# Transposes of the values placed between fill chunks, one gate chunk and the convolution taps placed anew, in the two sparse layers

## The reference, cut to what matters

```python
def second_block(x, meta_tokens, w_in, conv_w, conv_b, conv_ln_g, conv_ln_b, w_out, post_ln_g, post_ln_b):
    ...
    for l in range(DEPTH_2):                                   # 2 layers, 272 tokens, width 1024
        proj = jnp.einsum('bld,de->ble', h, w_in[l])
        a, g, zc, q, k, v, za, qi, ki, wi = jnp.split(proj, IN_SPLITS, axis=-1)
        y_conv = conformer_conv_branch(a, g, zc, ...)           # 31 taps per channel, layer norm, silu, * silu(zc)
        q, k, qi, ki = (rope of each)
        y_attn = dsa_sparse_attention(q, k, v, qi, ki, wi, topk) * jax.nn.silu(za)   # 68 best keys of each query
        y = jnp.einsum('ble,ed->bld', jnp.concatenate([y_conv, y_attn], axis=-1), w_out[l])
        h = layer_norm(DEEPNORM_ALPHA * h + y, post_ln_g[l], post_ln_b[l])
```

## Time and profile before

| what | value |
|---|---|
| median of the three timed runs | 986.49 us (986.46, 988.08, 986.49) |
| profiled execution, its own time | 985.01 us |
| its span, first to last instruction | 982.9 us |
| PE busy | 904.8 us, 92% of the span |
| POOL busy | 616.8 us, 63% |
| DVE busy | 518.4 us, 53% |
| ACT busy | 474.6 us, 48% |
| share of PE in the chain that ended last | 78% |

### The profile page before, as it was taken

How to read it: one execution, slowest core, us unless ns; L and a number is a source line. 1 busy time by engine, 2 the same in 40 slices (tenths; PEclk the granted TensorE clock), 3 DMA queues, 4 the chain that set the end, 5 groups by cost and what they waited for, 6 DMA issues and landing times.

```text
span 982.9 us, 16872 instructions
## 1 busy us (share of the span) xinstructions
PE 904.8 (92%) x6758; PEld 846.1 (86%) x6758; DVE 518.4 (53%) x1084; ACT 474.6 (48%) x941; POOL 616.8 (63%) x356
## 2 busy tenths in 40 slices
PE   3999899979999999899999997999988979998985
PEld 2986588879987989799999997999967979997885
DVE  5213011039962743755433014688994549899655
ACT  4535555542335554554444444445457564444673
POOL 4521344445455399799999988766771868765051
PEclk9999999999998999899999998999989989999997
DMA  9522532342433145546564665555420417545001
GB/s 255 159 75 86 177 124 86 89 127 87 129 114 102 43 145 162 166 139 203 174 199 136 188 198 149 172 143 161 129 87 1 133 53 217 172 129 172 1 1 43
DMA packets 133992, 125.97 MB, mean 128 GB/s; under 512 B 6406, under 2 KB 131963, under 8 KB 133915
## 3 DMA queue, kind: packets, MB, share of 16 engines
q1 hardware_dynamic: 133360, 124.17, 41.0%
q10 hardware_dynamic: 554, 0.73, 0.2%
HBM read 123.70 MB, written 1.05 MB: 127 GB/s over the span
## 4 chain that ended last, share of the span: by engine, by line
PE 78%; DVE 8%; ACT 5%; POOL 4%; DMA 3%; issue 2%; SPq 0%; ACTq 0%; DVEq 0%
PE PS L574 21%; PE PS L576 20%; PE PS L575 20%; PE PS L811 3%; POOL w_lo L1054 3%; DMA ring<-in_w_in 3%; PE PS L565 2%; ACT w_hi L1170 2%; PE PS L779 1%; PE PS L948 1%; PE PS L920 1%; PE PS L977 1%; DVE zoneB L1884 1%; DVE zoneB L1612 1%; DVE PS L1829 1%
## 5 line engine op out<-in xcount | busy, mean ns | idle before, releaser
L1054 POOL TENSOR_TENSOR w_lo<-ring,w_hi 128x1024 fp32r<-128x1024 f32 (+1 forms) x235 | 539.9, 2311 | 291.4 <-ACT w_hi L1170 278.6
L574 PE MATMUL PS<-x_hi,w_hi 128*128 128x256 f32 (+2 forms) x1560 | 460.2, 295 | 29.6 <-POOL x_lo L1064 9.3
L576 PE MATMUL PS<-x_hi,w_lo 128*128 128x256 f32 (+2 forms) x1560 | 447.1, 287 | 0.0
L575 PE MATMUL PS<-x_lo,w_hi 128*128 128x256 f32 (+2 forms) x1560 | 446.0, 286 | 0.0
L574 PEld LDWEIGHTS PS<-x_hi,w_hi 128*128 128x128 f32 (+1 forms) x1560 | 297.1, 190 | 38.7 <-issue 30.1
L575 PEld LDWEIGHTS PS<-x_lo,w_hi 128*128 128x128 f32 (+1 forms) x1560 | 296.5, 190 | 1.4 <-issue 0.2
L576 PEld LDWEIGHTS PS<-x_hi,w_lo 128*128 128x128 f32 (+1 forms) x1560 | 296.7, 190 | 0.0
L1170 ACT ACTIVATE w_hi<-ring 128x1024 fp32r<-128x1024 f32 (+1 forms) x231 | 233.4, 1013 | 84.6 <-PE PS L576 78.9
L1153 ACT ACTIVATE zoneA<-PS 128x272 f32<-128x272 f32 (+4 forms) x80 | 31.7, 397 | 154.9 <-PE PS L576 153.9
L1829 DVE SCALAR_TENSOR_TENSOR PS<-zoneA,cols,PS 128x256 f32<-128x256 f32 x240 | 98.4, 480 | 0.1
L1153 ACT ACTIVATE zoneB<-PS 128x256 f32<-128x256 f32 (+5 forms) x131 | 44.6, 367 | 89.7 <-DVE PS L1796 39.4
(11 more groups left out here) (269 smaller groups left out, 1241.0 us busy)
## 6 DMA issues: line engine op xcount, KB each, us to landing
ring<-in_w_in SPq DMA_DIRECT2D x58, 1024.0 KB, 5.5
ring<-in_w_ffn_in SPq DMA_DIRECT2D x22, 1024.0 KB, 5.1
ring<-in_w_out SPq DMA_DIRECT2D x12, 1024.0 KB, 5.2
ring<-in_w_ffn_out SPq DMA_DIRECT2D x16, 704.0 KB, 4.6
ring<-in_w_mla_o SPq DMA_DIRECT2D x4, 1024.0 KB, 5.2
ring<-in_w_hg_o SPq DMA_DIRECT2D x4, 1024.0 KB, 5.2
ring<-in_w_kv_b SPq DMA_DIRECT2D x2, 1024.0 KB, 5.4
ring<-in_w_q_b SPq DMA_DIRECT2D x2, 768.0 KB, 4.6
```

The costliest lines, as they stand in the source:

```text
L574: mm(out_, hi_w, hi_x, start=start, stop=False)
L575: mm(out_, hi_w, lo_x, start=False, stop=False)
L576: return mm(out_, lo_w, hi_x, start=False, stop=stop)
L1054: sub(lo_w, src, hi_w, ALU.subtract).then_inc(sem("w_lo"), 1)
```

## The change

Three things in each sparse layer, and no change in what is computed.

- The three groups of value transposes, and ACT's three copies of them, move from behind the rope stage into it: behind ropes 3, 4 and 5.
- ACT issues one exponential on a scratch column (`warm`) behind chunk 6 of the rope stage, so that the exponential's table is loaded there.
- Gate chunk za2 moves from attention step 9 to step 1 (za3 stays in the last step), and the 32 taps are split over the ten steps as 2, 8, 2, 3, 3, 3, 2, 3, 3, 3 instead of 3, 3, 3, 3, 4, 3, 3, 3, 3, 4.

```diff
 def z_chunks(l, s):
 
-    n = DSA_N[l] + DSA_LAG + 1
-    m = 8 - Z_EARLY
-    return [("zc" if z < 4 else "za", z % 4) for z in range(Z_EARLY + s * m // n, Z_EARLY + (s + 1) * m // n)]
+    return {1: [("za", 2)], DSA_N[l] + DSA_LAG: [("za", 3)]}.get(s, [])
+
+
+TAPS_AT_ATT = [0, 2, 10] + [10 + 22 * (_s - 1) // 8 for _s in range(2, 10)]
+TURN_AT = {3: 0, 4: 1, 5: 2}
...
-    ORDER += [part(f"L{_l}{n}", i) for n, i in [("qi", 1), ("qi", 2), ("qi", 3)] + IDX_FIRST + IDX_FILL + ROPE_FILL]
-    ORDER += [(f"L{_l}vt", i) for i in range(3)]
+    ORDER += [part(f"L{_l}{n}", i) for n, i in [("qi", 1), ("qi", 2), ("qi", 3)] + IDX_FIRST + IDX_FILL]
+    for _i, (_n, _m) in enumerate(ROPE_FILL):
+        ORDER += [part(f"L{_l}{_n}", _m)] + ([(f"L{_l}vt", TURN_AT[_i])] if _i in TURN_AT else [])
...
                     rope("q", 8 * l + i, q2[:, i, q_from:L] if i < 4 else k2[:, i - 4, :], 4)
-                out_of_psum(pe, *part(f"{T}v", 3))
-                for x, (t0, n) in enumerate(KEY_CHUNKS):
-                    g = CHUNK[f"{T}vt", x]
-                    bank_free(g)
-                    for c in range(4):
-                        last = nc.tensor.transpose(PS[0:n, BANK[g], c * P:(c + 1) * P], vT2[:, c, t0:t0 + n], ident)
-                    done(last)
+                    if i in TURN_AT:
+                        t0, n = KEY_CHUNKS[TURN_AT[i]]
+                        g = CHUNK[f"{T}vt", TURN_AT[i]]
+                        bank_free(g)
+                        out_of_psum(pe, *part(f"{T}v", 3))
+                        for c in range(4):
+                            last = nc.tensor.transpose(PS[0:n, BANK[g], c * P:(c + 1) * P], vT2[:, c, t0:t0 + n], ident)
+                        done(last)
...
                 for i, (n, m) in enumerate(ROPE_FILL):
                     take_proj(n, m)
+                    if i in TURN_AT:
+                        rows = KEY_CHUNKS[TURN_AT[i]][1]
+                        take(f"{T}vt", TURN_AT[i], v2[0:rows, TURN_AT[i], :], rows=rows, n=512)
+                    if i == 6:
+                        warm(ACT.Exp)
...
-                for x, (t0, n) in enumerate(KEY_CHUNKS):
-                    take(f"{T}vt", x, v2[0:n, x, :], rows=n, n=512)
...
                     if s < CLN_STEP[l]:
-                        a_, b_ = (at + x * (CC * TAPS - at) // CLN_STEP[l] for x in (s, s + 1))
-                        taps(a_, b_)
+                        taps(*(at + (TAPS_AT_ATT + [CC * TAPS - at])[x] for x in (s, s + 1)))
```

## The result

The changed kernel takes 989.81 us (median of 7 runs, 988.76 to 993.26); the kernel before, measured beside it, takes 985.63 (985.11 to 988.08). The ratio is 1.0042, with a 95% interval of 1.0027 to 1.0057: **slower by 4.2 us**. The profiled execution took 989.12 us with a span of 987.3, against 985.01 and 982.9.

A forecast was written before the change was run, and what follows sets the result against it. PE was taken to bound the kernel, with DVE the bound in the first ten attention steps. L0's +3.15 and L1's +0.65 sum to +3.8 us, from the median 986.49 to 990.3; range 987.1 to 992.7.

The forecast's parts named there:

- Transposes, 0.77 us a group: Rope stage: each moved group of four transposes delays PE 0.77 us, 2.3 for three groups; lower bound 1.2.
- Last rope product +2.1 and +1.75: End of the rope stage: DVE's last rope product comes 2.1 us later in L0 and 1.75 in L1.
- Table load 0: Rope stage, chunk 6: the moved exponential table load lies in ACT's waits, cost and gain 0.
- Gate chunk out of step 9, -1.2: Attention step 9: without za2 the copy of the taps follows at once, -1.2 us in L0, -1.05 in L1.
- L1's mean +0.65: L1 attention: early gate chunk costs nothing, mean begins 0.65 us later; bounds -0.45 and +1.9.
- L0: the wait for POOL's low part until 723.8: L0 attention step 1: za2 must wait for its low part, which POOL has ready at 723.8.
- The chunk 5.2 us: L0 attention step 1: za2 begins at the lower clock and takes 5.2 us; bounds 3.0 and 5.45.
- The third mask at 729.65, the mean +3.15: L0 attention: DVE's third mask comes at 729.65 behind za2, the mean at 741.05 against 737.89, +3.15 us.
- The split is worth nothing of itself: Attention steps: DVE has 32 taps before and after; the eight in step 1 only fill its wait for za2.
- the first (PE keeps the upper clock in L0): L0: PE keeps or at once regains the upper clock, chunk 3.0 us; total +1 to +1.6, 987.8; chance 0.17.
- The fourth, that L1 pays too: L1: PE waits through the eight taps, clock falls, later steps run lower; +1 to +2 more, 991.8; chance 0.10.
- The third: L0's mask on DVE is caught behind POOL's low parts; +1.65 us on the forecast, 992.0; chance 0.12.

The follow-up runs named there:

- e6_taps_even: The changed kernel with the taps split evenly as before, 6 instead of 10 ahead of the third mask; ratio 1.0103 to the kernel before.
- e1_late_gate: The changed kernel with gate chunk za2 back in step 9 and the old split of the taps; ratio 1.0012 to the kernel before.
- e2_turn_last: The changed kernel with the value transposes back behind the rope stage; early chunk, new split and moved table load stay; ratio 1.0034 to the kernel before.
- e9_fill_mean: The changed kernel with 14 small matrix products ahead of PE's wait before the mean, in both layers; ratio 1.0041 to the kernel before.
- e8_fill_wait: The changed kernel with 44 small matrix products ahead of za2's wait for POOL's low part in L0; ratio 1.0029 to the kernel before.
- e3_low_early: The changed kernel with POOL writing za2's low part in L0 behind the first of four groups of taps; ratio 1.0041 to the kernel before.
- e11_end_fill: e4_both with four small products ahead of each of the last two waits for exponentials, both layers; ratio 0.9982 to the kernel before, median 985.27 us.
- e4_both: The changed kernel with the transposes back behind the rope stage and za2's low part written early in L0; ratio 0.9999 to the kernel before.
- e10_low_fill: e4_both with 14 small matrix products ahead of the mean's wait; ratio 0.9995 to the kernel before.

## Why the prediction was right, step by step

It forecast 990.3, slower, by a sum of +3.8; the measured medians differ by 4.2 and the two spans by 4.4. The direction and its main cause were right: the early chunk waits for POOL in L0 and meets the lower clock there, and the last rotations come later. That the size agrees so well is luck. What the sum forecast, up to the mean of each layer, measured +2.49 in L0 (1.29 + 1.20) and -0.18 in L1 (1.01 - 1.19), +2.31 in place of +3.80. The other +2.09 of the 4.40 lies behind the means (1.69 + 1.51 - 1.11), where the sum had nothing, and is the lower clock in L0's mean and in L1's za3. The terms one by one:

- *Transposes, 0.77 us a group.* Mis-sized: 0.43 measured. The term that failed is the 0.59 from the last transpose to the chunk's second matmul, taken from a place near 63 us. In the rope stage the chunk's first matmul begins 0.35 behind the first transpose and the second 0.21 behind that. The lower bound of 1.2 for three was the better value (1.29).
- *Last rope product +2.1 and +1.75.* So too large. In L0 it is 715.97 instead of 714.87, +1.1; in L1 it comes 142.68 us behind L0's turning instead of 141.84, +0.84.
- *Table load 0.* Right, and the first exponential is still released by DVE; alone it measured 0.9988 with 1 inside the interval, which leaves room for a gain of 0.2%.
- *Gate chunk out of step 9, -1.2.* Right: with the old split e6_taps_even has 13.05 us from third mask to mean, e1_late_gate with the late chunk 14.23, a difference of 1.18.
- *L1's mean +0.65.* Its parts were -1.05, +1.75 and a rest; measured -0.18, most of the difference from the cheap transposes. "PE's clock falls there" happened, inside the chunk, and cost nothing up to the third mask, since DVE had ten taps to do.
- *L0: the wait for POOL's low part until 723.8.* Right: 724.08, released by POOL, behind 5.93 us of idle PE with the clock at 0.5 from 720.1.
- *The chunk 5.2 us.* 4.4 here, mis-sized by 0.8. The forecast counted 4.9 us from the chunk's start to the upper clock; here it was 2.8. What the two places have in common is the stretch at the lower clock: by the windows 603.9 to 610.8 us in the kernel before, 720.1 to 726.9 here, 6.8 us each. The chunk of the earlier trace rows began 1.9 us into it, za2 4.0. Nor is that length fixed: in e2_turn_last and e9_fill_mean the clock stayed at 0.50 for 10.2 us (722.0 to 732.2 and 722.5 to 732.7), and the chunk took 5.61 and 5.60 us, a little over the upper bound of 5.45. With the filling it took 3.1, beside the lower bound of 3.0.
- *The third mask at 729.65, the mean +3.15.* 728.90 and +2.49.
- *The split is worth nothing of itself.* For L0 the remark that the eight taps fill DVE's wait for za2 was the point: without it the mean is 1.57 us later.
- *Missing: the mean itself at the lower clock, +1.69.* The prediction took the mean's start as what the layer moves by, and its length and all behind it as fixed. That holds in eight of fourteen profiles in L0 (20.51 us each time) and not in the other six (22.0 to 23.0).

Of the rivals, the first (PE keeps the upper clock in L0) did not occur of itself, and made to occur (e8_fill_wait) it was worth 1.2 us up to the mean, against 2.2 in its sum. The fourth, that L1 pays too, came in this profile in another form: not in the steps with taps but in za3, for 1.51 us, of which 1.11 was taken back ahead of the end. In the form forecast it came in e3_low_early and e8_fill_wait, for 0.8 us, below its +1 to +2. The third didn't come in the changed kernel (the first mask is there at 721.37, ahead of the forecast 722.95); what e3_low_early met is of its kind. What made up for the dear transposes was the unforeseen mean: 4.18 at L0's turning where 3.15 was forecast at its mean.

## What to carry to other kernels

A chunk moved into a gap must have its inputs by then: ask which engine writes the last of them, and in what order, before looking at the gap. A fall of the clock is dear where a dense piece of matmuls follows a thin stretch (1.3 to 2.5 us here for 24 matmuls). Filling the idle time just ahead with products that nothing reads is worth a trial; with two of the four tried here (e8_fill_wait, e11_end_fill) the fall seen without them was absent, each in one profile. It is judged by many runs, because the mean clock differs between runs of the same code (0.965 to 0.972 over the first 23 of the kernel before). With gains of a microsecond, compare profiles milestone by milestone, and trust only what repeats: here the 2.4 us of the six groups of transposes did, and the clock did not. And measure the reference beside every comparison: the median of the kernel before moved by 1.9 us, from 985.63 to 987.57.

## What the runs showed of the hardware

- The granted clock is not settled by the matmuls just ahead alone. Around za3 in L1 the windows of before and after show the same work within 0.02 us a window, and the clock falls in one, some 2 us after the thin stretch's end, and not in the other. The Trainium skill says ("TensorE: Matmul & The Clock Gate", section "What's actually happening") that the chip's watch on activity runs freely and doesn't start with the kernel, so that the same kernel varies from run to run; these two sets of windows agree. What decides it in this kernel was not measured.
- Where one fall was prevented, another came later. With the clock held up to the mean, by the filling in e8_fill_wait or by the early low part in e4_both and e10_low_fill, za3 of L0 ran at 0.5 in all three; where it had fallen at the masks and the mean was normal, za3 of L0 was at 1.00 in seven profiles of nine. Only the filling right ahead of za3 went with both at 1.00, in one profile.
- The time from the chunk's start at the lower clock to the upper one was 2.8 us in the changed kernel and 4.9 in the earlier trace rows, in stretches of the lower clock of 6.8 us each.
- A product of DVE with both operands in SBUF took 1.32 us instead of 0.44 beside an operation of POOL in e3_low_early, and ended 0.3 us behind it; its neighbour reading PSUM was unchanged at 0.45.
- The start of L0's last rotation varied between 715.31 and 718.11 us over six profiles of kernels that are alike up to there, more than most edits in this study moved. In the three late ones (e1_late_gate, e6_taps_even, e9_fill_mean, 717.73 us and later) the clock was also at 0.50 for some 3 us from about 115 us on, in the three early ones (716.35 us and earlier) it was at 1.00 there. Windows of PE in e6_taps_even, then in the changed kernel:

```profile
116.00:118.00 2.00, 2.00 (x11) 0.50 0.33 58
...
116.00:118.00 2.00, 2.00 (x16) 1.00 0.90 275
```
